# State products of a state-space layer: both groups of a pair in one full-array matmul, the skip term in the strip of kernels

## The chip, the cores and the metric

The kernel runs on one core of a Trainium2 chip. The metric is the device time of one execution in microseconds (us). The matrix engine (TensorE) is called PE in the profile and its weight loads PEld; DVE is the vector engine, ACT the scalar engine, POOL the third elementwise engine, SP the engine that issues most transfers. SBUF is the working memory with 128 partitions; PSUM is the accumulation memory with 8 banks, `ps[:, bank, column]` in the code.

## What is computed

One encoder layer over 272 positions (16 meta tokens and 256 tokens) of width 2048: norm, a wide input product, neighbourhood attention, a bidirectional state-space branch, gates, an output product and a convolution-gated feed-forward part. All is float32. The change lies in the state-space branch, cut here to what matters:

```python
def s5_branch(u, ..., d_skip, w_glu):
    ug = u.reshape(b, L, 64, 16)                 # 64 groups of 16 channels, 64 complex states each
    y = (s5_direction(ug, ..., reverse=False)    # Re(C x_t), x_t = lam_bar * x_{t-1} + B_bar u_t
         + s5_direction(ug, ..., reverse=True)
         + ug * d_skip.reshape(64, 16))
    y = gelu(y.reshape(b, L, 1024))
    return y * sigmoid(y @ w_glu)
```

## The kernel before

**Dense products.** Nearly all time goes to products of the activations with weights that stream in from memory. A unit of weights (512 KB) is loaded by SP, split into a high and a low part by ACT (`hi_unit`, L501) and by DVE or POOL (`lo_unit`, L505), and then used by `half_unit` (L1468 to L1470): three matmuls of 128x128 weights with 258 columns for each weight tile. Rings of four units tie the engines together by semaphores.

**The scan.** The 272 positions are cut into 68 chunks (`NCH`) of 4 (`CHUNK`). DVE runs the recurrence over chunks for all 64 groups and both directions at once. The states lie in `X`, shape [128, NCH + 1, 128]: partition = real or imaginary part of a state, then the chunk, and last the 128 pairs of direction and group. So the states of one group at successive chunks lie 128 floats apart.

**The stage that is changed** has eight tiles `t` of 128 channels, that is 8 groups or `PB` = 4 pairs of groups. Its order on the matrix engine is written out by hand, one tile of it between halves of dense products: half a unit for tile t+1, `chunk_out(t)`, `kernels(t + 1)`, the other half unit.

- `kernels(t)` (L1612) multiplies tables `R1` and `Gn` into a strip in PSUM bank 2: for each pair the 16x16 matrices by which an input at one place of a chunk acts on an output at another, for 7 lags (`LAGS`, index `CHUNK - 1` is lag zero).
- `strip_out(t)` on DVE (L1195) multiplies the strip by `gmask`, which keeps the blocks of equal group, and writes it to `strip` in SBUF; it signals `s_st`. It waits for `s_kps` (kernels made) and `s_yps` (the last tile's products done).
- `chunk_out(t)` waits for `s_st` and, from the second tile on, for `s_ysb`. First the state products (L1625): for each of 4 pairs, 2 directions and 2 groups one matmul with 64 columns of `Gn` as weights and 68 states of `X` as the streamed operand, into the partition half of the group, `ps[64 * g:64 * g + 64, 4 + b, 0:NCH]`; for the backward direction the output is written in reverse. Then the strip products (L1631), 32 of 32 rows by 64 columns on the chunk's inputs `un`, added to the same places. It signals `s_yps`.
- `y_out(t)` on DVE (L1202) adds d times the input: four operations, one for each pair, from PSUM and `U2` into `U2`; it signals `s_ysb`. ACT then takes gelu of `U2` in place (L773, signal `s_yge`), and SP stores `U2` to memory (`y_store`), from where it is loaded back in another order for the gate product.
- `g_make(t)` on DVE makes the tables `Gn` of tile t (four multiplications, L1000, and an addition, L1121), in a ring of three; `kernels(t)` waits for it by `s_gm`.

DVE's order in the stage is: after the scan `strip_out(0)`, `g_make(1)`; then for each t `lo_unit`, `y_out(t)`, at t = 2 and 6 a `gate_block` (L965, which waits for the dense half units of the next tile), `strip_out(t + 1)`, `g_make(t + 2)`. ACT does `hi_unit` and then the gelu. After the stage `meta_scores` waits for `s_ysb` too, since it uses the same banks.

Of the kernel before, what the change touches and what calls it, by code (L numbers as in the profile page):

```python
# [17 lines left out]
GROUP = 16  # L18
# [9 lines left out]
P = 128  # L28
# [15 lines left out]
CHUNK = 4  # L44
# [23 lines left out]
def encoder_block(nc, tokens, gain_cols, ssm_params, skip_cols, conv_cols, b_rows, c_rows, near_bias, w_in, w_glu,  # L68
# [16 lines left out]
    with ctx:  # L85
# [7 lines left out]
        def keep(name, shape, dt=F):  # L93

            t = nc.alloc_sbuf_tensor_at(name, shape, dt, offset=cursor[0])
            cursor[0] += (int(np.prod(shape[1:])) * 4 + 31) // 32 * 32
            return t
# [23 lines left out]
        sgm = keep("half_signs", [P, 2])  # L121
        arena = (cursor[0] + 31) // 32 * 32
# [27 lines left out]
        dcol = at("d_columns", 82432, [P, PAIRS])  # L150
# [103 lines left out]
        s_ysb = sem("y_copied")  # L254
# [337 lines left out]
        def _(act):  # L592
# [177 lines left out]
            for t in range(KH):  # L770
                hi_unit(act, U_G + 4 * G_SCAN + DEPTH, t)
                act.wait_ge(s_ysb, t + 1)
                act.activation(U2[:, PB * t:PB * (t + 1), :], U2[:, PB * t:PB * (t + 1), :],  # L773
                               ACT.Gelu_apprx_tanh).then_inc(s_yge, 1)
# [159 lines left out]
        def _(dve):  # L934
# [256 lines left out]
            def strip_out(t):  # L1191
                dve.wait_ge(s_kps, t + 1)
                if t:
                    dve.wait_ge(s_yps, t)
                dve.tensor_tensor(strip[:, :, :, :].rearrange("p g l c -> p (g l c)"), ps[:, 2, 0:2 * LAGS * GROUP],  # L1195
                                  gmask[:, :, :, :].rearrange("p g l c -> p (g l c)"), ALU.mult).then_inc(s_st, 1)

            def y_out(t):
                dve.wait_ge(s_yps, t + 1)
                for b in range(PB):  # L1200
                    pair = PB * t + b
                    last = dve.scalar_tensor_tensor(out=U2[:, pair, :], in0=U2[:, pair, :], scalar=dcol[:, pair:pair + 1],  # L1202
                                                    in1=ps[:, 4 + b, 0:NCH], op0=ALU.mult, op1=ALU.add)
                last.then_inc(s_ysb, 1)

            three_and_one = ps[:, 0:4, 0:NL].rearrange("p (a b) n -> p a b n", b=2)[:, ::-1, 1, :]
            strip_out(0)
            g_make(1)
            dve.wait_ge(s_lo, U_G + DEPTH + 4 * G_SCAN)
            for t in range(KH):  # L1210
                lo_unit(dve, U_G + DEPTH + 4 * G_SCAN, t)
                y_out(t)
                if t % 4 == 2:
                    dve.wait_ge(s_used, U_G + 4 * G_SCAN + t + 2)
                    gate_block(gate_na, 2 * (G_SCAN + t // 4), three_and_one if t == 2 else ps[:, 0:2, 0:NL])
                if t + 1 < KH:
                    strip_out(t + 1)
                if t + 2 < KH:
                    g_make(t + 2)
# [232 lines left out]
        def _(pe):  # L1452
# [164 lines left out]
            def chunk_out(t):  # L1617
                pe.wait_ge(s_st, t + 1)
                if t:
                    pe.wait_ge(s_ysb, t)  # L1620
                for b in range(PB):
                    for d in range(DIRS):
                        for g in range(2):
                            o = ps[64 * g:64 * g + 64, 4 + b, 0:NCH]
                            mm(o[:, ::-1] if d else o, Gn[:, t % GSLOTS, d, 2 * b + g, :],  # L1625
                               X[:, 0:NCH, GROUPS * d + TG * t + 2 * b + g], start=d == 0, stop=False, skip_group_check=True)
                for j in range(CHUNK):
                    for b in range(PB):
                        rs = slice(32 * b, 32 * b + 32)
                        for g in range(2):  # L1630
                            ins = mm(ps[64 * g:64 * g + 64, 4 + b, 0:NCH],  # L1631
# [25 lines left out]
            def meta_scores():  # L1657
                pe.wait_ge(s_ysb, KH)
# [196 lines left out]
def layouts(inputs):  # L1855
# [6 lines left out]
    skip = a["ssm_d"][0].reshape(PAIRS, 2, 1, GROUP).transpose(1, 2, 3, 0)  # L1862
# [6 lines left out]
        "skip_cols": np.broadcast_to(skip, (2, CHUNK, GROUP, PAIRS)).reshape(P, PAIRS),  # L1869
# [26 lines left out]
```

## Time and profile before

| what | value |
|---|---|
| median of 3 runs | 1463.76 us (1461.24 to 1464.51) |
| profiled execution, its own time | 1463.71 us |
| its span in the trace | 1462.0 us |
| granted clock of the matrix engine, mean | 0.997 |
| busy: matrix engine, DVE, ACT, POOL | 99%, 41%, 45%, 69% |
| the changed stage | about 307 to 369 us |

The profile is of one execution. Busy times overlap; a matmul's duration contains the pipeline's depth, so that several are in flight at once, and their pace is read from starts. Each float32 matmul (not the split ones of L1468 to L1470) leaves two records. "128*64" in a row is the weights' rows by columns, "128x68" the streamed operand.

### The profile page before, as it was taken

What the parts mean: (1) busy time and instruction counts of PE and PEld (TensorE: products, weight loads), DVE (VectorE), ACT (ScalarE), POOL (GpSimd) and SP (SyncE); (2) the same over time, 40 slices, a digit from 0 to 9 for tenths busy, and PEclk for the clock granted to TensorE, in tenths of its full rate; (3) what the DMA queues carried; (4) which work ended last, traced back from release to release, by engine and by line L of the source; (5) the groups of instructions that cost most, each with busy time, mean ns of one, the idle gap of its engine ahead of it and who ended that gap; (6) DMA issues with size and microseconds to landing.
All of it is one profiled execution on the core that took longest, in us unless ns stands there. A gap on an engine that the chain in (4) does not pass through costs nothing.

```text
span 1462.0 us, 30268 instructions
## 1 busy us (share of the span) xinstructions
PE 1441.5 (99%) x11735; PEld 1373.0 (94%) x11735; DVE 603.3 (41%) x1147; ACT 663.3 (45%) x897; POOL 1013.9 (69%) x475
## 2 busy tenths in 40 slices
PE   9899999999999999999999999999999999999997
PEld 9899999998998999999999999999999998888886
DVE  7758888887545255543322222222222221003002
ACT  7346544432453554454544444444444443334333
POOL 5000058840678688898888888888888887888885
PEclk9999999999999999999999999999999999999999
DMA  8895456655665455665565655555555556555553
GB/s 290 237 222 182 136 173 203 185 155 144 189 195 181 134 174 183 231 213 178 176 191 181 186 183 178 184 186 177 183 186 182 179 185 201 187 187 178 196 187 130
DMA packets 238305, 271.50 MB, mean 186 GB/s; under 512 B 21904, under 2 KB 224016, under 8 KB 237456
## 3 DMA queue, kind: packets, MB, share of 16 engines
q1 hardware_dynamic: 227968, 257.11, 57.0%
q10 hardware_dynamic: 10256, 13.26, 2.8%
q8 instruction: 58, 0.95, 0.3%
q14 instruction: 23, 0.19, 0.0%
HBM read 262.07 MB, written 8.26 MB: 185 GB/s over the span
## 4 chain that ended last, share of the span: by engine, by line
PE 89%; DVE 4%; DMA 2%; issue 2%; ACT 1%; POOL 1%; DVEq 1%; SPq 0%; ACTq 0%; POOLq 0%
PE ps L1468 23%; PE ps L1470 22%; PE ps L1469 22%; PE ps L1789 6%; PE ps L1788 6%; PE ps L1787 6%; PE ps L1625 1%; DMA w_raw<-in_w_in 1%; DVE w_lo L505 1%; POOL w_lo L505 1%; PE ps L1568 1%; DMA x_feature_major<-in_tokens 1%; PE ps L1631 0%; DVE square_ring L956 0%; PE ps L1698 0%
## 5 line engine op out<-in xcount | busy, mean ns | idle before, releaser
L505 POOL TENSOR_TENSOR w_lo<-w_raw,w_hi 128x1024 fp32r<-128x1024 f32 x409 | 985.2, 2416 | 379.5 <-ACT w_hi L501 379.3
L501 ACT ACTIVATE w_hi<-w_raw 128x1024 fp32r<-128x1024 f32 x464 | 489.9, 1060 | 654.4 <-PE ps L1470 456.9
L1468 PE MATMUL ps<-act_hi,w_hi 128*128 128x258 f32 (+2 forms) x2432 | 695.4, 286 | 7.7 <-DVE w_lo L505 6.5
L1470 PE MATMUL ps<-act_hi,w_lo 128*128 128x258 f32 (+2 forms) x2432 | 690.7, 284 | 0.0
L1469 PE MATMUL ps<-act_lo,w_hi 128*128 128x258 f32 (+2 forms) x2432 | 689.2, 283 | 0.0
L1468 PEld LDWEIGHTS ps<-act_hi,w_hi 128*128 128x128 f32 x2432 | 461.2, 190 | 14.3 <-issue 9.9
L1469 PEld LDWEIGHTS ps<-act_lo,w_hi 128*128 128x128 f32 x2432 | 461.8, 190 | 0.1
L1470 PEld LDWEIGHTS ps<-act_hi,w_lo 128*128 128x128 f32 x2432 | 460.3, 189 | 0.0
L1789 PE MATMUL ps<-w_lo,hidden_hi 128*128 128x512 f32 x352 | 140.3, 399 | 0.0
L1788 PE MATMUL ps<-w_hi,hidden_lo 128*128 128x512 f32 x352 | 138.7, 394 | 0.0
L1787 PE MATMUL ps<-w_hi,hidden_hi 128*128 128x512 f32 x352 | 138.3, 393 | 0.0
L1421 DVE TENSOR_TENSOR h_tokens<-out_tokens,ps 128x512 f32<-128x512 f32 x8 | 5.5, 685 | 204.6 <-PE ps L1789 204.3
L1392 DVE TENSOR_TENSOR ps<-ps,rstd 128x512 f32<-128x512 f32 x22 | 15.4, 699 | 164.7 <-PE ps L1470 164.7
L1788 PEld LDWEIGHTS ps<-w_hi,hidden_lo 128*128 128x128 f32 x352 | 66.1, 188 | 17.1
L505 DVE TENSOR_TENSOR w_lo<-w_raw,w_hi 128x1024 fp32r<-128x1024 f32 x55 | 67.0, 1225 | 35.0 <-ACT w_hi L501 33.3
L1787 PEld LDWEIGHTS ps<-w_hi,hidden_hi 128*128 128x128 f32 x352 | 66.1, 188 | 15.6
L1789 PEld LDWEIGHTS ps<-w_lo,hidden_hi 128*128 128x128 f32 x352 | 66.1, 188 | 15.2
L1379 DVE TENSOR_TENSOR ps<-ps,rstd 128x516 f32<-128x516 f32 x22 | 15.5, 703 | 153.4 <-PE ps L1470 153.2
L1468 PE MATMUL ps<-mixed_hi,w_hi 128*128 128x258 f32 x256 | 72.3, 283 | 0.0
L1470 PE MATMUL ps<-mixed_hi,w_lo 128*128 128x258 f32 x256 | 72.3, 282 | 0.0
L1000 DVE TENSOR_TENSOR ps<-scan_states,ps 64x128 f32<-64x128 f32 (+1 forms) x201 | 59.6, 297 | 6.8
L1470 PEld LDWEIGHTS ps<-mixed_hi,w_lo 128*128 128x128 f32 x256 | 48.4, 189 | 0.0
(233 smaller groups left out, 1507.5 us busy)
## 6 DMA issues: line engine op xcount, KB each, us to landing
w_raw<-in_w_up SPq DMA_DIRECT2D x176, 512.0 KB, 3.5
w_raw<-in_w_in SPq DMA_DIRECT2D x128, 512.0 KB, 4.0
w_raw<-in_w_down SPq DMA_DIRECT2D x88, 512.0 KB, 3.5
w_raw<-in_w_out SPq DMA_DIRECT2D x32, 512.0 KB, 3.4
w_raw<-in_w_proj_na SPq DMA_DIRECT2D x16, 512.0 KB, 3.4
w_raw<-in_w_proj_ssm SPq DMA_DIRECT2D x16, 512.0 KB, 3.4
w_raw<-in_w_glu SPq DMA_DIRECT2D x8, 512.0 KB, 3.4
xT<-in_tokens ACTq DMA_DIRECT2D x1, 2176.0 KB, 8.7
```

Of the source, the lines that this page charges most:

```text
L501: act.activation(slot(whi, k), slot(raw, k), ACT.Copy).then_inc(s_hi, 1)
L505: pool.tensor_tensor(slot(wlo, k), slot(raw, k), slot(whi, k).bitcast(F), ALU.subtract).then_inc(s_lo, 1)
L1000: dve.tensor_tensor(o, a, b, ALU.mult)
L1379: dve.tensor_tensor(two, two, rstd[:, 0:NL].unsqueeze(1).to_broadcast(scale), ALU.mult).then_inc(s_as, 1)
L1392: dve.tensor_tensor(two, two, rstd[:, 2:NL].unsqueeze(1).to_broadcast([P, 2, SEQ]), ALU.mult).then_inc(s_as, 1)
L1468: mm(o, slot(whi, k)[:, cols], xh[:, kt, lo:lo + n], start=kt == 0, stop=False)
L1469: mm(o, slot(whi, k)[:, cols], low, start=False, stop=False)
L1470: ins = mm(o, slot(wlo, k)[:, cols], xh[:, kt, lo:lo + n], start=False, stop=kt == units * UKT - 1)
L1568: ins = mm(ps[:, 4 + 2 * d + g, NCH * b:NCH * (b + 1)], WT[hs, d, b, :], U2[hs, PB * t + b, :], start=True, stop=True)
L1787: mm(o, ah[:, kt, ts], slot(whi, k)[:, cols], start=kt == 0, stop=False)
L1788: mm(o, al[:, kt, ts], slot(whi, k)[:, cols], start=False, stop=False)
L1789: return mm(o, ah[:, kt, ts], slot(wlo, k)[:, cols], start=False, stop=kt == FT - 1)
```

## The change

The two groups of a pair are taken together in the state products: 128 columns of `Gn` as weights, and the states of both groups side by side (2x68 = 136 columns) as the streamed operand, into all 128 partitions. Of the four blocks of the result, [group of the kernel] by [group of the states], two are used: partitions 64g to 64g+63, columns 68g to 68g+67. The strip products add to these blocks. The skip term d is no longer added by DVE: `strip_out` adds `eye * d` to the lag-zero kernels of the strip after masking, with a drain before it; `eye` is made from the identity by four copies before the stage's first `strip_out`. `y_out`, `s_ysb` and the table of d by pairs are gone; d comes as one column per tile. ACT reads the sums out of PSUM for the gelu, in two operations, one for each group, and `chunk_out` and `meta_scores` wait for that gelu.

```diff
+        eye = keep("same_channel", [P, 2, GROUP])
-        dcol = at("d_columns", 82432, [P, PAIRS])
+        dcol = at("d_columns", 82432, [P, KH])
-        s_ysb = sem("y_copied")
@@ scalar
                 hi_unit(act, U_G + 4 * G_SCAN + DEPTH, t)
-                act.wait_ge(s_ysb, t + 1)
-                act.activation(U2[:, PB * t:PB * (t + 1), :], U2[:, PB * t:PB * (t + 1), :],
-                               ACT.Gelu_apprx_tanh).then_inc(s_yge, 1)
+                act.wait_ge(s_yps, t + 1)
+                for g in range(2):
+                    rs = slice(64 * g, 64 * g + 64)
+                    last = act.activation(U2[rs, PB * t:PB * (t + 1), :], ps[rs, 4:4 + PB, NCH * g:NCH * (g + 1)],
+                                          ACT.Gelu_apprx_tanh)
+                last.then_inc(s_yge, 1)
@@ vector
                 dve.tensor_tensor(strip[:, :, :, :].rearrange("p g l c -> p (g l c)"), ps[:, 2, 0:2 * LAGS * GROUP],
-                                  gmask[:, :, :, :].rearrange("p g l c -> p (g l c)"), ALU.mult).then_inc(s_st, 1)
-
-            def y_out(t):
-                dve.wait_ge(s_yps, t + 1)
-                for b in range(PB):
-                    pair = PB * t + b
-                    last = dve.scalar_tensor_tensor(out=U2[:, pair, :], in0=U2[:, pair, :], scalar=dcol[:, pair:pair + 1],
-                                                    in1=ps[:, 4 + b, 0:NCH], op0=ALU.mult, op1=ALU.add)
-                last.then_inc(s_ysb, 1)
+                                  gmask[:, :, :, :].rearrange("p g l c -> p (g l c)"), ALU.mult)
+                dve.drain()
+                same = strip[:, :, CHUNK - 1, :]
+                dve.scalar_tensor_tensor(out=same, in0=eye[:, :, :], scalar=dcol[:, t:t + 1], in1=same,
+                                         op0=ALU.mult, op1=ALU.add).then_inc(s_st, 1)
+            for b in range(PB):
+                rs = slice(32 * b, 32 * b + 32)
+                dve.tensor_copy(eye[rs, :, :].rearrange("p g c -> p (g c)"), ident[rs, rs])
+            dve.drain()
             strip_out(0)
             g_make(1)
@@
                 lo_unit(dve, U_G + DEPTH + 4 * G_SCAN, t)
-                y_out(t)
@@ tensor
             def chunk_out(t):
                 pe.wait_ge(s_st, t + 1)
                 if t:
-                    pe.wait_ge(s_ysb, t)
+                    pe.wait_ge(s_yge, t)
                 for b in range(PB):
+                    o = ps[:, 4 + b, 0:2 * NCH].rearrange("p (g n) -> p g n", g=2)
                     for d in range(DIRS):
-                        for g in range(2):
-                            o = ps[64 * g:64 * g + 64, 4 + b, 0:NCH]
-                            mm(o[:, ::-1] if d else o, Gn[:, t % GSLOTS, d, 2 * b + g, :],
-                               X[:, 0:NCH, GROUPS * d + TG * t + 2 * b + g], start=d == 0, stop=False, skip_group_check=True)
+                        first = GROUPS * d + TG * t + 2 * b
+                        mm(o[:, :, ::-1] if d else o, Gn[:, t % GSLOTS, d, 2 * b:2 * b + 2, :].rearrange("p g s -> p (g s)"),
+                           X[:, 0:NCH, first:first + 2].rearrange("p n g -> p g n"), start=d == 0, stop=False,
+                           skip_group_check=True)
                 for j in range(CHUNK):
                     for b in range(PB):
                         rs = slice(32 * b, 32 * b + 32)
                         for g in range(2):
-                            ins = mm(ps[64 * g:64 * g + 64, 4 + b, 0:NCH],
+                            ins = mm(ps[64 * g:64 * g + 64, 4 + b, NCH * g:NCH * (g + 1)],
@@
             def meta_scores():
-                pe.wait_ge(s_ysb, KH)
+                pe.wait_ge(s_yge, KH)
@@ layouts
-        "skip_cols": np.broadcast_to(skip, (2, CHUNK, GROUP, PAIRS)).reshape(P, PAIRS),
+        "skip_cols": _by_partition(a["ssm_d"][0]),
```

## Rows read from the trace of the kernel before

**Rows 1.** The page, busy us, share of the span and instructions of each engine.
```profile
PE 1441.5 (99%) x11735; PEld 1373.0 (94%) x11735; DVE 603.3 (41%) x1147; ACT 663.3 (45%) x897; POOL 1013.9 (69%) x475
```

**Rows 2.** The page, the chain that ended last, share of the span by engine.
```profile
PE 89%; DVE 4%; DMA 2%; issue 2%; ACT 1%; POOL 1%; DVEq 1%; SPq 0%; ACTq 0%; POOLq 0%
```

**Rows 3.** Windows in us: per engine busy us and instructions, clock, DMA share, GB/s.
```profile
312.50:361.80 49.30, 48.29 (x941) 43.53 (x940) 42.17 (x78) 11.34 (x15) 2.13 (x5) 1.00 0.48 127
```

**Rows 4.** Waits from 306 to 370 us: who for whom, us, times, longest.
```profile
PE ps L1625 <- DVE lag_strip L1195: 1.1, 1, 1.1
```

**Rows 5.** Timeline from 312.3 us, one tile and more: start, us, engine, line, operation.
```profile
312.33 0.28 PE L1470 MATMUL ps<-act_hi,w_lo 128*128 128x258 f32 x1
...
312.55 2.68 PE L1625 MATMUL ps<-scan_states,g_nat 128*64 128x68 f32 x32
...
315.15 0.92 PE L1631 MATMUL ps<-u_features,lag_strip 32*64 32x68 f32 x64
...
316.00 0.64 PE L1612 MATMUL ps<-g_nat,b_states 128*32 128x128 f32 x16
...
316.38 0.87 DVE L1202 SCALAR_TENSOR_TENSOR u_chunks<-u_chunks,d_columns,ps 128x68 f32<-128x68 f32 x4
...
316.58 0.39 PE L1468 MATMUL ps<-act_hi,w_hi 128*128 128x258 f32 x1
...
317.16 0.38 DVE L1195 TENSOR_TENSOR lag_strip<-ps,group_mask 128x224 f32<-128x224 f32 x1
...
319.64 2.67 PE L1625 MATMUL ps<-scan_states,g_nat 128*64 128x68 f32 x32
```

**Rows 6.** Timelines at 126.3 and 703.3 us: float32 products with contiguous operands.
```profile
126.61 2.00 PE L1568 MATMUL ps<-u_chunks,w_tr 64*128 64x68 f32 x32
...
703.39 0.28 PE L1470 MATMUL ps<-act_hi,w_lo 128*128 128x258 f32 x1
...
703.51 0.59 PE L1768 MATMUL ps<-token_squares_out,ones 128*128 128x258 f32 x2
```

**Rows 7.** Groups by line and form: count, busy us, mean ns, idle before.
```profile
L1625 PE MATMUL ps<-scan_states,g_nat 128*64 128x68 f32 x256 | 21.4, 344 | 1.1 <-DVE lag_strip L1195 1.1
...
L1768 PE MATMUL ps<-token_squares_out,ones 128*128 128x258 f32 x2 | 0.6, 378 | 0.0
```

**Rows 8.** Timeline of DVE at 79 us: copies of the power tables.
```profile
79.06 0.45 DVE L1097 TENSOR_SCALAR pow_in_im<-powers,half_signs 128x256 f32<-128x256 f32 x1
...
79.43 0.45 DVE L1098 TENSOR_SCALAR pow_out<-input_powers,half_signs 128x256 f32<-128x256 f32 x1
```

**Rows 9.** Timeline of DVE around the start of the stage.
```profile
310.21 0.65 DVE L1180 TENSOR_TENSOR scan_states<-scan_states,ps 128x128 f32<-128x128 f32 x2
...
310.98 0.39 DVE L1195 TENSOR_TENSOR lag_strip<-ps,group_mask 128x224 f32<-128x224 f32 x1
...
313.85 1.23 DVE L1121 TENSOR_TENSOR g_nat<-g_nat,t 128x1024 f32<-128x1024 f32 x1
```

**Rows 10.** Groups of small operations on DVE and ACT.
```profile
L773 ACT ACTIVATE u_chunks<-u_chunks 128x272 f32<-128x272 f32 x8 | 3.5, 432 | 37.1 <-DVE u_chunks L1202 37.1
...
L985 DVE TENSOR_TENSOR k_meta<-ps,rstd 128x32 f32<-128x32 f32 x4 | 0.7, 178 | 0.0
...
L1049 DVE COPY token_scale_by_partition<-ps 128x2 f32<-128x2 f32 x1 | 0.2, 160 | 0.5 <-PE ps L1510 0.5
...
L837 ACT ACTIVATE glu_ring<-ps 128x258 f32<-128x258 f32 x8 | 2.4, 383 | 0.0
```

**Rows 11.** The chain in order of time before the last tile: start, us, what.
```profile
360.83 0.04 DVE gate_na L965
...
361.44 0.39 DVE lag_strip L1195
...
361.88 2.67 PE ps L1625 x32
```

**Rows 12.** Group of DVE: the reduction over tiles of squares.
```profile
L956 DVE TENSOR_REDUCE square_ring<-norm_ring 128x272 f32<-128x1088 f32 x2 | 4.3, 2136 | 0.1
```

More of the change, by code:

```diff
@@ L1861, in layouts @@
     by_state = np.stack([v.transpose(2, 0, 1).reshape(STATE, DIRS * GROUPS) for v in lam_step], axis=1)
-    skip = a["ssm_d"][0].reshape(PAIRS, 2, 1, GROUP).transpose(1, 2, 3, 0)
     b = [v[0].transpose(2, 0, 1, 3).reshape(STATE, DIRS * GROUPS, GROUP) for v in (a["ssm_b_re"], a["ssm_b_im"])]
```

## The prediction

> **What bounds the kernel now.** I read the page first: the matrix engine is busy for 1441.5 of 1462.0 us, no other engine over 69% [rows 1], and the chain that ended last lies on it for 89% [rows 2]. So a change counts by the matrix-engine time that it takes out or puts in, and by waits of that engine. Next the window of the changed stage, 312.5 to 361.8 us: DVE is busy 42.17 of 49.30 us, ACT 11.34, and the matrix engine sat idle for about 1 us [rows 3]. The waits of the stage say where that 1 us is: one wait for lag_strip, 1.1 us, before the last tile [rows 4]; it is the only line there in which a matmul waits. Then one tile in order of time [rows 5]. The reader is to see three blocks between one dense matmul (L1470, start 312.33) and the next (L1468, start 316.58): the state products (L1625, 32 records), the strip products (L1631, 64), the next tile's kernels (L1612, 16). Each float32 matmul of the program leaves two records. What the edit can move on the matrix engine is the stretch from 312.33 to the first L1631 at 315.15: 2.82 us in each of 8 tiles, 22.6 us in all.
>
> **State products.** Now there are 16 per tile, each 128 rows by 64 columns, streaming 68 states; the two groups of a pair go to the two halves of the array. They run side by side: 32 records last 2.68 us from the first start to the last end, a record 0.344, so the 16 pairs start (2.68-0.34)/15 = 0.156 us apart [rows 5, 7]. After the change 8 products of 128 by 128 stream 136 states: 16 records, one after the other. Call the pitch of such a record S. Before is 16 pairs of 0.156 and 0.32 around them. A first reading is that the work is the same: as many columns read (2x68), half of the result thrown away. The question is what sets 0.156. Two rows with contiguous operands: the 32 records of L1568, 68 columns too, in pairs on two row halves, take 2.00 us in all, 0.68 less than those of L1625; and one full-array float32 product of 258 columns (L1768) has its second record 0.59-0.378 = 0.21 behind the first, 0.82 ns a column [rows 6, 7]. So neither 68 columns nor a weight load explains 0.156. What differs in L1625 is its streamed operand, X[:, 0:NCH, q]: neighbours lie 128 floats apart, and both streams read all 128 partitions. That costs 156/68 = 2.29 ns per column of a stream, or 1.15 ns per element read by the two together.
>
> S is bounded so. Below: a strided read costs a lone stream nothing, 0.82 x 136 = 112 ns. Above: each stream pays 2.29 ns a column by itself, S = 2.29 x 136 = 312 ns. Between: the two streams share what is slow, so that 136 elements cost what they cost now, 156 ns, or a little less without a second stream. The nearest other strided read is DVE's of the power tables (L1097, L1098, neighbours 256 floats apart): 256 elements every 0.36 us, overhead included, 1.4 ns each [rows 8]. With the contiguous L1121, 1024 elements in 1.23 us [rows 9], they lie on one line of (1.23-0.36)/768 = 1.13 ns an element; a lone strided stream is not slowed to 2.29 there. I take S = 148 ns: 156 is what these 136 elements cost in this very place, and a fifth of the way down to 112 is granted because no second stream interferes. L1625 is the nearest row, the same operand, stride and count.
>
> The change of tile shape costs something as well. L1470 to L1625 takes 0.22 us where dense matmuls are 0.12 apart, and a full-array float32 product follows a dense matmul after 0.12 (703.39 to 703.51) [rows 5, 6]. So the first new product starts 0.12 after L1470, and the extra 0.09 comes only before the strip products. The Trainium skill (TensorEngine Tiling (Array Packing), Key Properties) says that changing the tiling mode, though not the tile, drains the engine; the trace agrees, with these 0.22 against 0.12 us.
>
> A tile then takes 0.12 + 16 S + 0.09 where it took 2.82: a saving of 2.61 - 16 S, with S = 0.148 that is 0.24 us, and 1.94 us in 8 tiles.
>
> **Strip and d.** The mask product of the strip (0.38 us) is followed by a drain and an operation on 128x32 elements. From the end of L1180, 310.86, to the start of L1195, with a drain between, are 0.12 us [rows 9], and 128x32 took 0.178 [rows 10]; the two overlap a little, so 0.25 us more before each s_st, between 0.18 and 0.3. Seven of the eight are covered: the strip for tile 1 ends at 317.54 and is wanted at 319.64 [rows 5], and the others likewise. The last is not: gate_block, strip, products stand in one line, and the matrix engine waits for it now [rows 11]. That is +0.25 us. That tile has no dense matmul right before it, so it also loses the saved change of shape: +0.1.
>
> **Start of the stage.** Four copies of 32x32 and a drain go ahead of strip_out(0): small operations took 0.16 to 0.18 [rows 10], so 0.5 to 0.8, I take 0.65. Strip 0 was ready at 311.37 and becomes ready at 311.37 + 0.65 + 0.25 = 312.3, while the products begin at 312.45: hidden, by 0.15. But g_make(1) ends 0.9 later, at 315.98 instead of 315.08 [rows 9], and kernels(1), which began at 316.00, would now begin at 315.76: +0.2. In later tiles g_make has more than 1 us to spare, and DVE gets time back:
>
> **y_out** goes: four operations, 0.87 us per tile on DVE [rows 5]. Nobody on the matrix engine waited for it [rows 4], so this is worth nothing. **Gelu** becomes two ACT operations on 64 partitions of 272 elements each out of PSUM. Partitions don't shorten an operation; 272 took 0.43 from SBUF, 258 took 0.38 from PSUM [rows 10], so 2 x 0.4 instead of 0.87 + 0.43. U2 is ready a little sooner, and banks 4 to 7 are wanted 3.5 us later. ACT is busy a quarter of the time, and SP's stores, queued behind it, move with it. Nothing. Smaller skip_cols: nothing.
>
> **Sum:** -1.94 + 0.25 + 0.1 + 0.2 = -1.4 us. Profiled 1463.71 (span 1462.0 and 1.7 around it), median of the three runs 1463.76: both become 1462.3 to 1462.4; I take 1462.4.
>
> **The rivals.**
> (a) The array is the bound for a lone stream: S = 112 ns. Then 2.61 - 1.79 = 0.82 per tile, 6.5 in all; the wait for g_make(1) grows by 0.6 to 0.8, the other two stay: -6.5 + 0.8 + 0.35 = -5.35, 1458.4 us. For it: one stream instead of two that fight, and DVE's strided reads go at DVE's own pace. Against: 1.15 ns per element is already slower than the array needs, and that is measured in this very place.
> (b) Slower: each strided element holds up its own stream. Pairs ran side by side, so putting them in one stream doubles their time: S = 312 ns, 16 S - 2.61 = +2.38 per tile, +19.1 in all, 1483.4 with the terms above (0.55). A milder form goes by the reduction L956, which reads 1088 elements at a stride of 272 floats in 2.14 us [rows 12], 1.97 ns each: S = 267, +13.3, 1477.6. It decides from S over 181 ns, or 1.33 ns a column. For it: that reduction. Against: L1097 and L1098, whose elements cost half of that.
> The Trainium skill (SBUF — State Buffer, the note on SBUF "cachelines" under the port table) says that every access to a new 16-byte line pays a penalty and that two hits per line are needed for full bandwidth. By that rule the new products pay for each of 136 columns in one stream, and it is on the side of (b); that L1625 is slower than L1568 agrees with it, the size it leaves open.
> (c) Only the other terms act: S = 163 ns, where products and change of shape cancel, gives 1464.3. It is part of my own case.
>
> **How the numbers follow.** A comparison of this kernel can tell about 0.2% (2.9 us) from no change. Faster by that means 8(2.61 - 16 S) - 0.55 > 2.9, S under 136 ns; slower means S over 181. Chances: my case (S 137 to 181, 1461 to 1466.6) 0.40; (a) with its neighbourhood up to 136 ns 0.38; (b) 0.22, of which a third lies between 181 and 250 ns. The range must take in (a), with half a us for its terms and the scatter of the runs, so 1457.5, and the first third of (b), up to 1473 (S about 230); over that lies about 0.15. My case alone: 1460.5 to 1466.5.
>
> **What would show it.** In the changed profile: the state products as 16 records of 128x128, 128x136 per tile, (whole - one)/15 is S directly; the stretch from the last L1470 to the first strip product 2.58 us (a: 2.00, b: 4.5 to 5.2); a wait of kernels(1) for g_nat of about 0.2 us in the first tile; the wait for lag_strip at the end 1.3 to 1.4 us instead of 1.1; DVE's busy time in the stage down by about 5 us with no effect. The prediction fails if S is not between 137 and 181, or if ACT's two gelus appear as a wait on the matrix engine.

## The result, and the profile after

The changed kernel takes 1474.9 us (median of 6 runs, 1471.2 to 1478.1), the kernel before 1463.1 (6 runs beside them): a ratio of 1.0086, interval 1.0074 to 1.0098. It is slower by some 12 us. The forecast was 1462.4 with no change that can be measured; the time lies 1.9 us over the upper end of the range, and of the rivals the mild form of (b) is nearest (S = 267 ns, 1477.6).

The page, busy us of each engine, against [rows 1]:
```profile
PE 1452.1 (99%) x11607; PEld 1380.7 (94%) x11607; DVE 600.0 (41%) x1127; ACT 666.4 (45%) x905; POOL 1013.2 (69%) x475
```
The matrix engine has 10.6 us more (1441.5 before). DVE's relief is there too, 48.8 us busy in the stage before and 45.3 after where some 5 less were forecast, and is worth nothing. Where the 10.6 went is seen in the timeline of one tile, start and us, that answers to [rows 5]:
```profile
330.37 0.29 PE L1472 MATMUL ps<-act_hi,w_lo 128*128 128x258 f32 x1
330.50 3.89 PE L1627 MATMUL ps<-scan_states,g_nat 128*128 128x136 f32 x16
334.31 0.92 PE L1634 MATMUL ps<-u_features,lag_strip 32*64 32x68 f32 x64
335.17 0.65 PE L1614 MATMUL ps<-g_nat,b_states 128*32 128x128 f32 x16
335.74 0.39 PE L1470 MATMUL ps<-act_hi,w_hi 128*128 128x258 f32 x1
```
From the last dense record to the first strip product are 330.37 to 334.31, 3.94 us; it was 2.82, and 2.58 were forecast. The strip products (0.92) and the kernels (0.65) are what they were. The 16 records of L1627 last 3.89 in all, one 0.41, so they start (3.89-0.41)/15 = 232 ns apart. Record by record, leaving out the first interval of a tile, it is 231 to 234 in all eight tiles. S is 233 ns, where 148 were assumed and 181 was the point from which the change loses. S is the pitch of one record, and a float32 matmul leaves two: here and below "a product" with a pace in ns, per product or per element, is one record, and a whole matmul takes twice that.

The waits of the stage, who for whom, us, times, longest, against [rows 4]:
```profile
DVE lag_strip L1198 <- PE ps L1614: 8.3, 5, 2.5
DVE gate_na L968 <- PE ps L1472: 8.1, 2, 4.1
...
PE ps L1627 <- DVE lag_strip L1202: 1.7, 2, 1.4
```
The matrix engine waits for DVE 1.7 us in the stage, where it waited 1.1; DVE now waits for the matrix engine. So at most 0.6 us of the loss is a wait.

**The stage added up.** I take the stage from the first record of kernels(0) to the first of meta_scores. It lasts 60.93 us before (307.47 to 368.40) and 71.35 after (308.58 to 379.93), +10.42. What follows it is the same length in every kernel of this study (1093.6 to 1093.7 us); what comes before it differs between profiles by up to 4 us with nearly the same code (the stage begins between 305.45 and 309.55), so the tables below go by the length of the stage, and the verdicts by the timed runs. The 10.42 are: 8 tiles x (3.94-2.82) = 8.96; the start, 0.5; tile 3, 0.2; the last tile, 0.5 (0.33 for its strip, 0.09 for the shape change that it can't save, 0.08 in the first interval of its products) and 0.25 for a strip block of 1.17 instead of 0.92. That is 10.4, all of it.

The two profiled executions lie 11.75 us apart. Of the rest 1.1 us lie before the stage, and much of what differs there goes with the clock: the stage begins at 305.45 in the one profile whose clock never fell to 0.50 between 55 us and the stage (innermost_y_out), at 305.7 to 308.3 in the six where it fell for 3.4 us (before among them), and at 308.3 to 309.6 in the six where it fell for 6.8 us (after among them). Two windows of after, granted clock third from the right:
```profile
62.60:65.80 3.20, 3.20 (x16) 3.20 (x16) 2.90 (x12) 2.11 (x2) 0.00 (x0) 0.50 0.57 178
137.70:140.90 3.20, 2.76 (x12) 2.76 (x13) 3.20 (x7) 0.09 (x1) 0.00 (x0) 0.50 0.57 164
```

The rows for the four small ones, timelines of DVE and the matrix engine:
```profile
311.56 0.65 DVE L1183 TENSOR_TENSOR scan_states<-scan_states,ps 128x128 f32<-128x128 f32 x2
...
312.33 0.74 DVE L1208 COPY same_channel<-ident 32x32 f32<-32x32 f32 x4
...
313.14 0.39 DVE L1198 TENSOR_TENSOR lag_strip<-ps,group_mask 128x224 f32<-128x224 f32 x1
...
313.44 0.28 PE L1472 MATMUL ps<-act_hi,w_lo 128*128 128x258 f32 x1
...
313.61 0.25 DVE L1202 SCALAR_TENSOR_TENSOR lag_strip<-same_channel,d_columns,lag_strip 128x32 f32<-128x32 f32 x1
...
314.01 3.94 PE L1627 MATMUL ps<-scan_states,g_nat 128*128 128x136 f32 x16 [0.29 <-DVE lag_strip L1202]
...
337.48 0.70 DVE L968 TENSOR_TENSOR gate_na<-ps,rstd 128x516 f32<-128x516 f32 x1 [4.08 <-PE ps L1472]
...
338.09 0.38 DVE L1198 TENSOR_TENSOR lag_strip<-ps,group_mask 128x224 f32<-128x224 f32 x1
...
338.55 0.25 DVE L1202 SCALAR_TENSOR_TENSOR lag_strip<-same_channel,d_columns,lag_strip 128x32 f32<-128x32 f32 x1
...
338.59 0.28 PE L1472 MATMUL ps<-act_hi,w_lo 128*128 128x258 f32 x1
...
338.85 3.97 PE L1627 MATMUL ps<-scan_states,g_nat 128*128 128x136 f32 x16
...
371.12 0.38 DVE L1198 TENSOR_TENSOR lag_strip<-ps,group_mask 128x224 f32<-128x224 f32 x1
...
371.58 0.25 DVE L1202 SCALAR_TENSOR_TENSOR lag_strip<-same_channel,d_columns,lag_strip 128x32 f32<-128x32 f32 x1
...
371.89 3.96 PE L1627 MATMUL ps<-scan_states,g_nat 128*128 128x136 f32 x16 [1.41 <-DVE lag_strip L1202]
...
375.78 1.17 PE L1634 MATMUL ps<-u_features,lag_strip 32*64 32x68 f32 x64
```
Start: the scan ends at 311.56+0.65 = 312.21; the strip's mask product starts 0.93 later instead of 0.12 (four copies, 0.74, and a drain), and the d operation adds 0.33 (313.53 to 313.86). The products should have followed the dense record of 313.44 by 0.12 and came 0.57 behind it, 0.45 late, and their first interval is 0.27 instead of 0.22. Tile 3: gate_block (L968) holds the strip back, it is ready at 338.80, and the products start 0.26 behind the dense record instead of 0.12, and their first interval is 0.30 instead of 0.22. Last tile: the strip, 0.33 longer by the d operation (371.50 to 371.83), stands alone on the path, as forecast.

The 0.25 of the last strip block is the clock. Windows of the last tile, with the granted clock third from the right:
```profile
373.80:375.70 1.90, 1.90 (x9) 1.72 (x8) 0.00 (x0) 0.00 (x0) 0.00 (x0) 0.50 1.07 302
...
377.00:378.00 1.00, 1.00 (x9) 1.00 (x10) 0.00 (x0) 0.97 (x3) 0.00 (x0) 1.00 0.08 29
```
The matrix engine had been idle for 1.41 us before L1627 and then busy; the clock fell to 0.50, which is the level of 1.2 GHz, from 373.1 to 376.5, and the strip block took 1.17 us. The state products did not notice: their pitch there is 231 to 234 ns, as at full clock. So these 233 ns are not a fixed number of the engine's clock cycles.

### The profile page after: what moved, and what is told of

The parts are those of the page before. It is cut to its first block, busy times and chain, and to the rows that moved or that the text cites. A ratio compares the mean times of both kernels' runs of the same rounds, so it can differ in the third digit from the quotient of the medians.

```text
span 1473.6 us, 30009 instructions
## 1 busy us (share of the span) xinstructions
PE 1452.1 (99%) x11607; PEld 1380.7 (94%) x11607; DVE 600.0 (41%) x1127; ACT 666.4 (45%) x905; POOL 1013.2 (69%) x475
## 4 chain that ended last, share of the span: by engine, by line
PE 81%; DVE 9%; DVEq 3%; issue 2%; DMA 2%; ACT 1%; POOL 1%; SPq 0%; ACTq 0%; POOLq 0%
PE ps L1470 20%; PE ps L1472 19%; PE ps L1471 19%; PE ps L1790 6%; PE ps L1792 6%; PE ps L1791 6%; DVE ps L1003 3%; DVE scan_states L1183 3%; PE ps L1627 2%; DMA w_raw<-in_w_in 2%; DVEq L1182 2%; DVE w_lo L505 1%; POOL w_lo L505 1%; PE ps L1570 1%; PE ps L1634 0%
## 5 line engine op out<-in xcount | busy, mean ns | idle before, releaser
L1470 PE MATMUL ps<-act_hi,w_hi 128*128 128x258 f32 (+2 forms) x2432 | 696.3, 286 | 8.1 <-DVE w_lo L505 4.9
L1472 PE MATMUL ps<-act_hi,w_lo 128*128 128x258 f32 (+2 forms) x2432 | 690.9, 284 | 0.0
L1470 PEld LDWEIGHTS ps<-act_hi,w_hi 128*128 128x128 f32 x2432 | 461.7, 190 | 15.0 <-issue 8.5
L1472 PEld LDWEIGHTS ps<-act_hi,w_lo 128*128 128x128 f32 x2432 | 460.7, 189 | 0.0
L1470 PE MATMUL ps<-mixed_hi,w_hi 128*128 128x258 f32 x256 | 72.6, 283 | 0.0
L1472 PE MATMUL ps<-mixed_hi,w_lo 128*128 128x258 f32 x256 | 72.3, 282 | 0.0
L1472 PEld LDWEIGHTS ps<-mixed_hi,w_lo 128*128 128x128 f32 x256 | 48.3, 189 | 0.0
```

Of the source, the lines that this page charges most:

```text
L1470: mm(o, slot(whi, k)[:, cols], xh[:, kt, lo:lo + n], start=kt == 0, stop=False)
L1472: ins = mm(o, slot(wlo, k)[:, cols], xh[:, kt, lo:lo + n], start=False, stop=kt == units * UKT - 1)
```

## The experiments

The theory after this reading: a product that reads neighbours 128 floats apart takes its columns at the pace of that read, one stream at a time; before, two streams each paid that at the same time, and the change puts them in a row. The rivals: the width of the tile or the length of 136 columns is dear by itself; the reordered output is; and the d operation and gelu, not the products, make the loss.

**Sweep of the distance, full array.** The changed kernel with another distance between neighbours in each tile (so other states are read than the result needs, and these tiles write 136 columns in one run, not reversed; all else is computed):
```diff
+ flat = X[:, :, :].rearrange("p n g -> p (n g)")
- moving = X[:, 0:NCH, first:first + 2].rearrange("p n g -> p g n")
+ moving = flat[:, 0:2 * NCH * STEPS[t]:STEPS[t]]   # t: 0 3 4 5 6 -> 1 2 4 8 32
```
Tile 1 reads the right states with the group innermost (two neighbours, then a jump of 128) and writes them in that order, tile 2 reads so and writes by groups, tile 7 is as changed.


> The changed kernel with another streamed operand for the state products in each tile, so that one trace has the pitch S of all: tiles 0, 3, 4, 5, 6 stream 136 floats of X at a distance of 1, 2, 4, 8 and 32 floats (other numbers than the states, and no reversed output), tile 1 the true states with the group innermost (two neighbouring floats, then a jump of 128) into PSUM in that order, its strip products into every second column, tile 2 the same operand into PSUM by groups, tile 7 as changed. The output is not the reference's, as these tiles leave the true order out. Theory 1, the distance between streamed floats is the whole cost of 233 ns: tile 0 at 112 to 118, tiles 5, 6 and 7 at 233; by where it rises between 1 and 8 it tells how many floats of one fetch are needed; tiles 1 and 2 at 112 to 140 if two floats per fetch are enough, 170 to 233 if not. Theory 2, the full width does it (128 columns of float32 weights beside 136 streamed ones): 233 in all tiles, tile 0 too. Theory 3, the output in two pieces or in reverse does it: tiles 0, 3, 4, 5, 6 at 115, tile 2 at 233 or more, tile 1 at 115.


Timeline, state products of tiles 1, 3, 4 and 6:
```profile
318.12 2.03 PE L1640 MATMUL ps<-scan_states,g_nat 128*128 128x136 f32 x16
...
330.98 2.19 PE L1640 MATMUL ps<-scan_states,g_nat 128*128 128x136 f32 x16
...
338.24 4.05 PE L1640 MATMUL ps<-scan_states,g_nat 128*128 128x136 f32 x16
...
355.06 3.89 PE L1640 MATMUL ps<-scan_states,g_nat 128*128 128x136 f32 x16
```
The pitch from the starts of records: distance 1, 115.8 ns; 2, 120.0; 4, 243.5; 8, 246.7; 32, 233.3; 128 (tile 7), 232.5. Group innermost: 116.8, with the output by groups 116.6. One run took 1467.2 us.

**Sweep of the distance, pairs of half-width products.** The same in the kernel before (other states again), at distances 1, 2, 3, 4, 8 and 32 in tiles 0 to 5, the two streams of a pair one float apart; tile 6 leaves out the second group's state products, tile 7 is as before:


> The kernel before with the two streams of a pair at a distance of 1, 2, 3, 4, 8 and 32 floats in tiles 0 to 5 (other numbers than the states, so the output is not the reference's), tile 6 with the products of the first group of each pair alone (the second group's are left out), tile 7 as before. My prediction's sharing of one source by two streams: tile 0 at 57 to 60 ns a pair, tiles 4, 5, 7 at 156, tile 6 (a lone stream of 68) at 78 or down to 57. Theory 1, each stream pays by itself 1.71 ns a column as the changed kernel shows (233/136): a lone stream in tile 6 takes 68 x 1.67 + 5 = 118, and two streams side by side cost 156, so they disturb each other by a third only. Theory 2, strided reads are not the cause of 156: tile 0 at 156 too.


Timeline, tiles 0 (distance 1), 3 (4), 6 (a lone stream at 128) and 7 (as before):
```profile
312.50 1.18 PE L1632 MATMUL ps<-scan_states,g_nat 128*64 128x68 f32 x32
...
331.10 2.19 PE L1632 MATMUL ps<-scan_states,g_nat 128*64 128x68 f32 x32
...
351.48 2.06 PE L1632 MATMUL ps<-scan_states,g_nat 128*64 128x68 f32 x16
...
357.68 2.67 PE L1632 MATMUL ps<-scan_states,g_nat 128*64 128x68 f32 x32 [1.09 <-DVE lag_strip L1195]
```
Pitch of a pair: 60.0 ns at distance 1, 64.3 at 2, 94.2 at 3, 123.9 at 4, 126.2 at 8, 130.2 at 32, 155.5 at 128; the lone stream at 128, 116.7 a product of 68 columns. One run took 1459.5 us.

The two sweeps give the rule for these streams. A lone stream at distance 128 takes 116.7/68 = 1.72 ns per element with 68 columns, and 233/136 = 1.71 with 136: length and width don't matter. Contiguous it is 0.85. The rise lies between 2 and 4 floats, with 3 (seen in pairs alone) between: two elements in 16 bytes are full speed, one is half. The output's order costs nothing (116.8 and 116.6), and distances 4 to 32, whose output is in one run, are as slow as the changed kernel's. The Trainium skill (SBUF — State Buffer, the note on SBUF "cachelines") says that two hits per 16-byte line are needed for full bandwidth; the runs agree, and add the size, a factor of 2. And side by side pays: two streams at distance 4 to 32 need 124 to 130 ns for a pair where one product alone (at 128) needs 117. At 128 there is a second effect, 155.5, taken up below.

**Half of the change each.** products_only: the state products as changed, but d stays in y_out, which now needs 8 operations on half the partitions per tile. d_gelu_only: the products as before, d in the strip, y_out gone, gelu in one operation out of PSUM.


> The kernel before with the full-array state products alone; d and the copy stay on DVE (eight half operations per tile instead of four), gelu stays in SBUF. If the products are the loss: period of a tile 8.2 us where it was 7.09, so +9 us, 1472. DVE's second 0.87 us per tile is hidden by its slack unless the last tile shows it (y_out of tile 6 lies before the gate block, which waits for the matrix engine anyway). If the strip and gelu parts of the change cost the time, it is within 2 us of before.

> The changed kernel with the half-width state products of before, gelu as one operation from PSUM. My terms: +0.25 at the last tile, and at the start the copies of eye (0.81 us before strip 0, measured) with the strip's second operation (0.33) put strip 0 at 312.5 on the clock of before where the matrix engine asks for it at 312.45, and g_make(1) ends at 316.2 for 316.0: +0.1 and +0.2. Together +0.6 us, 1463.7 to 1464.5 beside 1463.1. A rival: freed DVE time is worth something, then 1 to 3 us under before. Another: these parts are what cost, +8 us or more.


Waits of the matrix engine, of products_only and then of d_gelu_only:
```profile
PE ps L1628 <- DVE lag_strip L1195: 1.3, 1, 1.3
```
```profile
PE ps L1624 <- DVE lag_strip L1199: 1.4, 1, 1.4
...
PE ps L1611 <- DVE g_nat L1121: 0.2, 1, 0.2
```
products_only: 1475.5 us (before 1463.7), ratio 1.0080 [1.0059, 1.0100], stage 70.71. d_gelu_only: 1464.7, ratio 1.0008 [0.9994, 1.0021], stage 61.91. So the products are the whole measurable loss (the expectation had 1472 for it, from a period of 8.2 us a tile, which is what the tiles take), and d with gelu costs a microsecond of the stage: the wait at the end 1.4 instead of 1.1, kernels(1) 0.2 late and kernels(4) 0.25 late behind g_make (the wait of L1611 shown is kernels(4)'s), the products of tile 3 0.05, and the start 0.15.

**The group innermost.** The cure for the full-array product: two groups' states lie side by side in X, so read them in that order and let PSUM take the same order.
```diff
- o = ps[:, 4 + b, 0:2 * NCH].rearrange("p (g n) -> p g n", g=2)
+ o = ps[:, 4 + b, 0:2 * NCH].rearrange("p (n g) -> p n g", g=2)
- X[:, 0:NCH, first:first + 2].rearrange("p n g -> p g n")
+ X[:, 0:NCH, first:first + 2]
- strip products and gelu: NCH * g:NCH * (g + 1)
+ strip products and gelu: g:2 * NCH:2
```


> The changed kernel with one thing undone that cost: the 136 states are streamed with the group innermost, two neighbouring floats and then a jump of 128, into PSUM in the same order; the strip products write, and the gelu reads, every second column. Same products, same numbers of everything. By the steps run (116.7 ns in its tile 1) a tile takes 0.12 + 16 x 0.117 + 0.1 = 2.09 us where the kernel before takes 2.82 and the changed one 4.05: -0.73 x 8 = -5.8 us against before, of which the start (0.35), the last tile (0.35) and the wait for g_make(1) (0.7) take 1.4: 1459 beside 1463.4, and 15.5 us under the changed kernel. Rival: every second column in PSUM slows the strip products or gelu; then the strip block is over 0.86 us and the gain under 2.


Timeline of a tile, and the waits:
```profile
327.05 2.03 PE L1627 MATMUL ps<-scan_states,g_nat 128*128 128x136 f32 x16
329.01 0.92 PE L1633 MATMUL ps<-u_features,lag_strip 32*64 32x68 f32 x64
```
```profile
PE ps L1627 <- DVE lag_strip L1202: 1.8, 1, 1.8
...
PE ps L1614 <- DVE g_nat L1124: 1.4, 2, 0.7
```
The pitch is 117 ns, the strip products that write every second column still take 0.92. 1462.1 us, ratio 0.9986 [0.9975, 0.9998] to before; stage 58.03. That is 13.3 us shorter than the changed kernel's, by reading the same states in another order. It is 2.9 and not the 4.4 expected shorter than before's (1459 us were expected): with shorter products the two kernels() of tiles 1 and 4 come before g_make is done (1.4 us), and the last strip keeps the engine 1.8 us.

Two variants of it. innermost_y_out puts y_out back (as in products_only); innermost_eye_early makes the four copies for the d operation earlier, ahead of the stage:


> The same products, but d and the copy stay on DVE as before the change (as eight half operations, 1.7 us a tile). If DVE's time is covered, this is as fast as group_innermost or 0.7 us faster, since strip and start terms are gone. If DVE has become the next bound, its work per tile, about 6.2 us before the change plus 0.87 for the halves = 7.1, exceeds the matrix engine's period of 6.35 and the gain is gone: 1463 to 1465. I expect the second, so that what I priced at nothing, y_out leaving DVE, is worth some us once the products are fast.

> group_innermost with the four copies of eye made long before the scan's end. If the start terms are real, it gains 0.3 (strip 0 no longer late) to 0.9 us (g_make(1) no longer late): 1458 to 1458.7. If they were hidden: no difference to group_innermost.


Waits of innermost_y_out:
```profile
PE ps L1628 <- DVE lag_strip L1195: 4.8, 7, 2.3
PE ps L1615 <- DVE g_nat L1121: 4.0, 6, 0.7
```
DVE is the bound there, with 13 waits of 8.8 us in all; stage 65.29, 1469.7 us, ratio 1.0043 [1.0027, 1.0058]. The direction is the one expected, the size is not: 1463 to 1465 were. Its y_out is twice as many operations as before's (1.7 us instead of 0.87 per tile), so how much of the 7.3 us is y_out itself and how much the doubling these runs don't tell apart. The early copies: stage 57.49, 0.54 less, inside the 0.3 to 0.9 expected: the products of tile 0 come 0.3 us sooner, kernels(1) waits 0.2 less. The start term is real. The time, 1460.0 us, ratio 0.9972 [0.9961, 0.9983], is 2.1 under group_innermost's; the stage accounts for a quarter of that.

**Two chunks side by side.** If 16 bytes must hold two wanted elements, X can be laid out so for half-width products too: [34, 128, 2], chunk pairs innermost. ACT's and DVE's copies into X become two each; d, gelu and the early copies as above.
```diff
- X = at("scan_states", 0, [P, NCH + 1, DIRS * GROUPS])
+ X = at("scan_states", 0, [P, NCH // 2, DIRS * GROUPS, 2])
- X[:, 0:NCH, q]
+ X[:, :, q, :]
```


> The half-width products of before, two streams side by side, but X laid out so that the states of two successive chunks are neighbours (chunk pair, group, chunk in the pair), d in the strip and gelu from PSUM as changed, eye early. Every fetch then serves two floats in a stream. By the steps run a pair of products at a distance of 1 took 60 ns and at 2 took 64, against 156: 16 x 0.093 = 1.5 us per tile, 12 us in 8 tiles, if nothing else becomes the bound; DVE's work per tile, 5.7 us, is then about the period of 5.6, so 8 to 11 us: 1453 to 1456. Rivals: the scan, whose operations now take every second float of a row, gets slower (over 1 us in all puts it on the chain), or ACT and DVE lose it at the copies of chunk inputs, which are now two operations instead of one.


A pair of products starts every 78.7 ns (155.5 before). DVE's scan reads and writes X two floats apart now and takes what it took (0.65 for two of L1188, as L1180 in [rows 9]). Stage 54.20, 1458.4 us, ratio 0.9955 [0.9940, 0.9970], short of the 1453 to 1456 expected: the pair takes 78.7 and not 60 to 64, and kernels() waits 2.4 us for g_make. But contiguous pairs start every 60.0, so 19 ns were open here too, as 155.5-117 = 38 were in before.

**What two streams take from each other.** The kernel before, with the distance of neighbours and the distance between the two streams changed by tile (other states, all else computed):
```diff
+ STREAMS = ((128, 4), (128, 32), (128, 0), (64, 1), (96, 1), (120, 1), (126, 1), (128, 1))
+ step, apart = STREAMS[t]
+ q = 8 * (DIRS * b + d) % 32 + apart * g
+ moving = flat[:, q:q + (NCH - 1) * step + 1:step]
```


> The kernel before with other places of X streamed by the pair of state products in each tile (the states of the true group are left out, the output is not the reference's). Open is why two streams at 128 floats take 155 ns a pair, when a lone one takes 117 and two at 4 or 8 floats 126. Tiles 0 to 2: distance 128, the second stream 4, 32 or 0 floats from the first; tiles 3 to 6: distance 64, 96, 120 and 126, the second 1 float from the first; tile 7 as in the kernel before but with other groups. Theory A, a clash of the two streams on the same fetch: tiles 0 and 1 at 126, tile 2 and 3 to 7 at 155. Theory B, the large power of two as distance: tiles 0, 1, 2, 7 (128) and 3 (64) at 155, tiles 4 to 6 (96, 120, 126) at 126. Theory C, neither: all at one value.


Groups by form in the windows of tile 0 (128 apart, streams 4 apart) and tile 2 (128, the same elements): count, busy us, mean ns:
```profile
L1630 PE MATMUL ps<-scan_states,g_nat 128*64 128x68 f32 x32 | 2.1, 296 | 0.0
...
L1630 PE MATMUL ps<-scan_states,g_nat 128*64 128x68 f32 x32 | 2.7, 343 | 0.0
```
(2.1-0.296)/15 and (2.7-0.343)/15; from the starts of records 119.1 and 156.2. Streams 32 apart: 118.7. With streams one float apart: 156.2 at a distance of 64, 153.6 at 128, but 127.7 at 96, 128.8 at 120, 130.7 at 126. Each of the two explanations was half right: the two streams hinder each other when they want the same 16 bytes at once, and by much (37 ns) only at distances of 64 and 128 floats; at 96, 120 and 126 it is 9 to 12 ns. That the second condition is a multiple of 64 is a guess from two distances, and it has no explanation here. The groups g and g+1 of a pair, which before reads at once, fulfil both.

**The order alone.** The kernel before, its 32 products in another order, so that the two at work read groups of different pairs, 5 or 3 floats apart and in different 16 bytes; nothing else:
```diff
- for b in range(PB):
+ for at_once in range(PB):
      for d in range(DIRS):
          for g in range(2):
+             b = (at_once + PB // 2 * g) % PB
```
chunk_pairs_reordered is chunk_pairs with the same two lines.


> The kernel before with its state products in another order and nothing else: beside the first group of pair b goes the second group of pair b+2, so that the two streams lie 5 floats apart and not 1. The run two_streams had 119 ns a pair for 4 or 32 floats apart, 156 for 0 or 1. 16 x 0.037 = 0.59 us per tile, 4.7 us in 8 tiles; DVE's 6.2 us per tile still fit in the period of 6.5: 1458 to 1460 beside 1463.5. If the clash is not between streams in flight together, nothing changes and the pitch stays 155.

> chunk_pairs with the same reordering; its pairs start 79 ns apart where two streams of contiguous floats take 60. If the rest is the same clash, 62 to 66 ns: 16 x 0.015 = 0.24 us per tile, at most 1.9 us, of which DVE's 5.7 us per tile leave 1 or less: 1457 to 1458.5. If 79 is the price of two floats per fetch in two streams, no change.


Timeline of a tile of reordered, and its windows in the last tile:
```profile
325.89 2.09 PE L1626 MATMUL ps<-scan_states,g_nat 128*64 128x68 f32 x32
327.91 0.92 PE L1632 MATMUL ps<-u_features,lag_strip 32*64 32x68 f32 x64
```
```profile
358.60:360.60 2.00, 1.93 (x32) 1.82 (x32) 1.59 (x2) 0.14 (x1) 0.67 (x2) 1.00 0.79 218
...
361.80:364.30 2.50, 2.50 (x14) 2.50 (x12) 0.87 (x4) 1.50 (x2) 0.00 (x0) 0.50 1.11 356
```
The same of chunk_pairs_reordered, and its waits:
```profile
325.37 1.18 PE L1629 MATMUL ps<-scan_states,g_nat 128*64 128x68 f32 x32
326.48 0.92 PE L1635 MATMUL ps<-u_features,lag_strip 32*64 32x68 f32 x64
```
```profile
PE ps L1615 <- DVE g_nat L1123: 3.0, 2, 1.7
...
PE ps L1629 <- DVE lag_strip L1207: 1.6, 1, 1.6
```
reordered: pitch 117 to 119, 1459.8 us, ratio 0.9972 [0.9960, 0.9985]; two lines that change no work. The products whose streams lie 3 floats apart start 118.2 ns apart, those at 5 floats 118.0: it is the same 16 bytes that clash, not a small distance. A tile takes 6.5 us instead of 7.1, as expected. The stage is 58.17, 2.76 shorter and not 4.7: 0.5 is a wait of kernels(4) for g_nat, and 1.4 is the clock, which in this profile fell to 0.50 from 360.9 to 364.3, after the idle 1.09 us of the last tile; dense matmuls there start 0.21 apart instead of 0.12. Before has the same idle 1.08 us and kept 1.00. chunk_pairs_reordered: pitch 60.3, stage 53.06, 1455.9 us, ratio 0.9947 [0.9933, 0.9961]. It is the fastest kernel here, faster than before and after; of the 8 x 16 x 18 ns = 2.4 us that the order takes out of chunk_pairs, 1.1 arrive: kernels() waits 3.0 us for g_make instead of 2.4, starts some 0.05 to 0.1 late in the other tiles, and the last strip keeps the engine 0.2 longer. The time is 1.1 us under the range expected, which the stage does not show.

The stages side by side, in us:

| kernel | pitch, ns per two groups | stage | ratio to before |
|---|---|---|---|
| before | 155.5 | 60.93 | 1 |
| after | 233 | 71.35 | 1.0086 |
| products_only | 233 | 70.71 | 1.0080 |
| d_gelu_only | 155.5 | 61.91 | 1.0008 |
| group_innermost | 117 | 58.03 | 0.9986 |
| innermost_y_out | 117 | 65.29 | 1.0043 |
| innermost_eye_early | 117 | 57.49 | 0.9972 |
| reordered | 118 | 58.17 | 0.9972 |
| chunk_pairs | 78.7 | 54.20 | 0.9955 |
| chunk_pairs_reordered | 60.3 | 53.06 | 0.9947 |

## Why the prediction was wrong

**The step that failed is the value of S.** The bounds were right: 112 from contiguous products (measured 115.8) and 312 from each stream paying 2.29 ns a column. So was the frame: with S = 233 the formula gives 8 x (16 x 0.233 - 2.61) = +8.94 and the stretches show +8.96. What failed was the choice between the ends. "The two streams share what is slow, so that 136 elements cost what they cost now" took the 155.5 as one shared queue of 136 elements. It was two queues of 68, each at 1.72 ns an element and both at once (117), and 38 ns more from a clash of neighbours. The lone stream of 68 columns (116.7, steps_tiled) shows the first part, streams 4 floats apart (119.1, two_streams) that side by side is nearly free. Rival (b) had the mechanism, "each strided element holds up its own stream", but took the clash for a part of it, and so 312.

**The row that misled** is DVE's of the power tables [rows 8], 1.13 to 1.4 ns an element at a distance of 256 floats. It was called the nearest strided read of a lone stream. It is one of another engine, and that engine's reads don't show what the matrix engine's do; that the reduction L956 at 1.97 [rows 12] disagreed with it was a sign that neither carries over. The comparison in the prediction itself, L1568 with 68 contiguous columns against L1625 [rows 6, 7], did show that the distance costs something, but it hid how much. L1568 lies on row halves, and its pairs start (2.00-0.32)/15 = 0.112 us apart; pairs on column halves, the shape of L1625, start 0.060 apart when contiguous (steps_tiled, tile 0). So the distance costs a pair a factor of 2.6 (2.0 of it for each stream, the rest the clash), and not the 1.4 that the rows seemed to say. Why contiguous row halves take nearly twice as long no run here shows. The Trainium skill's rule on 16-byte lines, cited there, was on the right side, and that side was given 0.22. Nothing in the trace of before had a lone strided stream on the matrix engine, so rows alone could not close it; but (a) and my case both need a lone stream that is much faster than one of a pair, that is, a limit that the two share, and no row showed one.

**"Seven of the eight are covered"** was wrong for one, besides the first: at t = 2 gate_block stands ahead of strip 3 on DVE, as it does at the last; +0.2. In d_gelu_only it is 0.05 there and 0.25 at kernels(4), whose g_make stands behind.

**Start of the stage.** Called hidden by 0.15; it cost 0.5. The terms were small: the copies with their drain 0.81 for 0.65, the d operation 0.33 for 0.25, together 1.14 for 0.90. The matrix engine also asked for the strip 1.35 us after the scan's end and not 1.59 as before, and from the strip's end to the first product are 0.15 us (313.86 to 314.01) that the sum did not have. The delay of g_make(1), 0.2, is there in d_gelu_only; in the changed kernel the longer products cover it.

**Last tile.** +0.35 forecast (0.25 and 0.1), 0.5 measured: 0.33 and 0.09, and 0.08 in the first interval after the wait; right in kind. The 0.25 of the clock was not foreseen. **Change of shape:** L1472 to L1627 takes 0.13 us where L1470 to L1625 took 0.22 [rows 5]; right. **Gelu:** no wait of the matrix engine for it in any kernel; right. **y_out** "is worth nothing": right for this kernel, whose products are long. It is nearly so at 118 ns too: reordered keeps its four operations, and the matrix engine waits 0.5 us for g_nat. Eight operations at that pitch are not covered (innermost_y_out), and four at 60 to 79 ns were not tried.

**What would have been seen with the right S.** Had the change read the group innermost, S would have been 117, close to rival (a), and the kernel 1462.1. The idea of one full-array product is therefore worth little even when it is read well (117 for a pair against 118 by order alone), because the halves already worked side by side. What the sum needed was one question ahead of all others: is the price of the pair one of the array, of one stream, or of both together?

## What to carry to other kernels

Before two tiled products are put in one, find out whether they ran side by side at a read-bound pace: then merging them puts two waits in a row. For float32 operands that the matrix engine streams, let every 16 bytes hold two wanted elements, by the order of the loops or the layout, and let streams at work at the same time read different 16 bytes. A price of one engine's strided read does not carry over to another engine; measure it there by a sweep of the distance, one tile each.

## What the runs showed that was not expected

- A lone strided float32 stream costs the matrix engine 1.71 ns per element at a distance of 32 or 128 floats, against 0.85 to 0.88 up to a distance of 2; at 4 and 8 floats it is a little more, 1.79 to 1.81 (243.5 and 246.7 ns). Why these are dearer than 32 is open.
- That pace doesn't follow the engine's clock: 231 to 234 ns a product at a granted clock of 1.00 and of 0.50. (An estimate: if contiguous columns, 0.85 ns at 1.00, take twice that at 0.50, they are as slow there, so this shows no more than that the read takes the same time at both. No run has contiguous columns of this shape at 0.50.)
- Two half-width strided streams side by side take 119 ns where one alone takes 117, unless both want the same 16 bytes at a distance of 64 or 128 floats (153.6 to 156.2); with the same 16 bytes at 96, 120 and 126 floats they take 127.7 to 130.7.
- Writing PSUM out of order cost the products nothing: the state products by turns into two runs 68 float32 columns apart 116.6 ns, in order 116.8; the strip products into every second column 0.92 us, as in order.
- After an idle stretch of 1.1 to 1.4 us in the last tile the clock fell to 0.50 for 3.4 us in the profiles of after, products_only, reordered and steps_full, and kept 1.00 in those of before, d_gelu_only and the others with as long an idle stretch or a longer one. The strip block took 1.17 to 1.32 us there instead of 0.92. What decides it is open. The window of steps_full:
```profile
365.40:368.60 3.20, 3.20 (x74) 2.82 (x72) 0.00 (x0) 0.00 (x0) 0.00 (x0) 0.50 0.89 256
```
